# Weights packed on the host in the order of the ring, one run of 4 KB per partition and load

## The reference

```
def hybrid_mixer(x, w_in, mix_scale, w_out, gdn_conv_w, ..., fox_f_bias):
    proj = jnp.einsum('btd,de->bte', x, w_in)          # w_in 1024 x 3218
    ...                                                # delta rule, convolutions, attention
    mixed = jnp.concatenate([o_a, o_b, o_c], axis=-1) * mix_scale
    return jnp.einsum('bte,ed->btd', mixed, w_out)     # w_out 1024 x 1024

def swiglu(x, w1, w3, w2):                             # dense: 1024 x 2816, 2816 x 1024
    h = jax.nn.silu(jnp.einsum('btd,df->btf', x, w1)) * jnp.einsum('btd,df->btf', x, w3)
    return jnp.einsum('btf,fd->btd', h, w2)

def moe_swiglu(x, w_router, w1, w3, w2):               # 8 experts: 1024 x 3584, 3584 x 1024
    ...
    def expert_block(args):
        xb, e = args
        h = jax.nn.silu(xb @ w1[e]) * (xb @ w3[e])
        return h @ w2[e]
```

## Time and profile before

| | before |
|---|---|
| median of 3 runs | 2567.8 us (2567.65 to 2568.49) |
| profiled execution: span | 2567.1 us |
| PE busy | 2380.6 us (93%) |
| DVE busy, ACT busy | 1618.7 us, 1226.7 us |
| DMA | 536.82 MB in 421,484 packets, 209 GB/s over the span |
| queue of SP (q1) | 61.0% of the 16 engines' time |
| chain that ended last | PE 85%, DVE 7%, ACT 3%, issue 3%, DMA 1% |

### The profile page before, as it was taken

How to read it: one execution, slowest core, us unless ns; L and a number is a source line. 1 busy time by engine, 2 the same in 40 slices (tenths; PEclk the granted TensorE clock), 3 DMA queues, 4 the chain that set the end, 5 groups by cost and what they waited for, 6 DMA issues and landing times.

```text
span 2567.1 us, 31674 instructions
## 1 busy us (share of the span) xinstructions
PE 2380.6 (93%) x11343; PEld 1937.9 (75%) x11343; DVE 1618.7 (63%) x1855; ACT 1226.7 (48%) x1315; POOL 188.2 (7%) x224
## 2 busy tenths in 40 slices
PE   7988899898879999999999999999699999997997
PEld 6777688785867878787877777778488778756886
DVE  3564554265548888888888888888654407523443
ACT  1222244104117777777777786867543312222432
POOL 2020000012120000000000000000290001000000
PEclk9998899999879999999999999999899989878999
DMA  7400555440019989898999998999456444223552
GB/s 253 128 1 1 164 180 180 142 153 27 1 41 343 364 309 362 307 365 307 364 307 357 305 367 304 364 312 365 152 182 196 152 153 143 99 70 103 180 181 80
DMA packets 421484, 536.82 MB, mean 209 GB/s; under 512 B 20126, under 2 KB 379432, under 8 KB 421288
## 3 DMA queue, kind: packets, MB, share of 16 engines
q1 hardware_dynamic: 414928, 523.21, 61.0%
q0 software_dynamic: 3168, 9.86, 1.2%
q10 hardware_dynamic: 3320, 2.82, 0.3%
HBM read 532.67 MB, written 3.15 MB: 209 GB/s over the span
## 4 chain that ended last, share of the span: by engine, by line
PE 85%; DVE 7%; issue 3%; ACT 3%; ACTq 1%; DMA 1%; DVEq 0%; POOL 0%; SPq 0%
PE bank L991 18%; PE bank L992 18%; PE bank L993 18%; PE bank L808 5%; PE bank L1164 4%; PE bank L968 2%; PE bank L1012 1%; PE bank L804 1%; PE bank L1074 1%; PE bank L1312 1%; PE bank L907 1%; PE bank L918 1%; PE bank L921 1%; PE bank L767 1%; PE bank L1295 1%
## 5 line engine op out<-in xcount | busy, mean ns | idle before, releaser
L1749 DVE TENSOR_TENSOR weights_lo<-ring_data,weights_hi 128x2048 fp32r<-128x2048 f32 x435 | 995.7, 2303 | 176.5 <-ACT weights_hi L1363 175.9
L1363 ACT ACTIVATE weights_hi<-ring_data 128x2048 fp32r<-128x2048 f32 x435 | 825.8, 1915 | 91.9 <-DMA ring_data<-in_moe_w 90.7
L991 PE MATMUL bank<-weights_hi,xg_hi 128*128 128x512 f32 x896 | 365.5, 408 | 1.5 <-DVE xg_lo L2094 1.5
L993 PE MATMUL bank<-weights_hi,xg_lo 128*128 128x512 f32 x896 | 353.5, 395 | 0.0
L992 PE MATMUL bank<-weights_lo,xg_hi 128*128 128x512 f32 x896 | 353.0, 394 | 0.0
L991 PE MATMUL bank<-weights_hi,hT_hi 128*128 128x512 f32 x712 | 282.7, 397 | 16.4 <-DVE hT_lo L1761 16.4
L1338 ACT ACTIVATE arena<-bank 128x384 f32<-128x384 f32 (+4 forms) x186 | 93.8, 523 | 426.7 <-PE bank L808 111.8
L992 PE MATMUL bank<-weights_lo,hT_hi 128*128 128x512 f32 x712 | 283.5, 398 | 0.0
L993 PE MATMUL bank<-weights_hi,hT_lo 128*128 128x512 f32 x712 | 279.4, 392 | 0.0
L1374 ACT ACTIVATE hT_hi<-bank 128x256 fp32r<-128x256 f32 x178 | 65.0, 384 | 346.0 <-PE bank L1012 345.6
L991 PE MATMUL bank<-weights_hi,xT_hi 128*128 128x512 f32 x528 | 214.8, 407 | 16.3 <-issue 16.3
(11 more groups left out here) (423 smaller groups left out, 2856.4 us busy)
## 6 DMA issues: line engine op xcount, KB each, us to landing
ring_data<-in_moe_w SPq DMA_DIRECT2D x672, 512.0 KB, 4.7
ring_data<-in_ffn_w_in SPq DMA_DIRECT2D x88, 512.0 KB, 4.7
ring_data<-in_w_in SPq DMA_DIRECT2D x70, 512.0 KB, 4.6
ring_data<-in_ffn_w SPq DMA_DIRECT2D x66, 512.0 KB, 4.2
ring_data<-in_ffn_w_out SPq DMA_DIRECT2D x44, 512.0 KB, 4.2
ring_data<-in_w_out SPq DMA_DIRECT2D x24, 512.0 KB, 4.4
ring_data<-in_w_in SPq DMA_DIRECT2D x8, 396.0 KB, 4.5
ring_data<-in_w_in SPq DMA_DIRECT2D x8, 390.0 KB, 6.7
```

The lines of the kernel that those rows point to most:

```text
L991: mm(o, x_hi, w_hi, start=start, stop=False, **kw)
L993: return mm(o, x_lo, w_hi, start=False, stop=stop, **kw)
L1363: nc.scalar.activation(f.hi_slot(f.n0 + at), f.ring.slot(f.n0 + at), ACT.Copy).then_inc(f.ring.hi_done, 1)
L1749: v.tensor_tensor(f.lo_slot(f.n0 + at), w, f.hi_slot(f.n0 + at), ALU.subtract).then_inc(f.ring.lo_done, 1)
```

## The change

The host writes all streamed weights into two arrays, `stream1` (first block) and `stream2` (second block), in the order in which the ring takes them. Each slot is 128 rows of 8 KB, row p holding what partition p gets, in the layout that the slot had before (narrow blocks are padded with zeros that are not loaded). `Ring.load` takes the slot's rows and issues two halves, each one run per partition: 4096 bytes for a full slot, 3168 or 3120 for the blocks of 198 and 195 columns. An up slot's halves were `w1` and `w3` before; now they are the first and the second two row blocks, with both weights in each. The number of DMAs, their sizes, the ring, the waits and everything on the other engines stay.

```diff
-    def load(self, sp, n, dst, src, more=0):
+    def load(self, sp, n, src, w=8 * FC, more=0):
...
-        half = dst.shape[1] // 2
-        if isinstance(src, tuple):
-            parts = [(dst[:, :, FC * i:FC * i + FC], src[i]) for i in range(2)]
-        else:
-            parts = [(dst[:, half * i:half * i + half, :], src[:, half * i:half * i + half, :]) for i in range(2)]
-        for d, r in parts:
-            sp.dma_start(d, r).then_inc(self.loaded[n % RING], 16)
+        slot, half = self.slot(n), w // 2
+        for i in range(2):
+            r = slice(half * i, half * i + half)
+            sp.dma_start(slot[:, r], src[:, r]).then_inc(self.loaded[n % RING], 16)
...
+            def slot_of(ring, n):
+
+                return a[("stream1", "stream2")[ring is ring2]][bass.ds(n * P, P), :]
...
-                    ring.load(sp, n0 + m, ring.slot(n0 + m)[:, 0:8 * w].rearrange("p (k c) -> p k c", k=DT), cols(a["w_in"][l], c, w))
+                    ring.load(sp, n0 + m, slot_of(ring, n0 + m), 8 * w)
...
+def slot_rows(w, c, n):
+
+    return w[:, c:c + n].reshape(-1, P, n).transpose(1, 0, 2).reshape(P, -1)
...
+def stream(slots):
+
+    out = np.zeros((len(slots), P, 8 * FC), np.float32)
+    for n, v in enumerate(slots):
+        out[n, :, 0:v.shape[1]] = v
+    return out.reshape(-1, 8 * FC)
```

More of the change, by code:

```diff
@@ L528, in rest, with dense @@
                     chunk(c, 0, r)
[L529 to L536, removed]
+                down(f, 0, f.down_at(f.chunks - 1), r, e)
+            def dense(f):
+                first(f)
+                rest(f)
             mixer(0)
-            dense(ffn, a["ffn_w1"][0], a["ffn_w3"][0], a["ffn_w2"][0])
+            dense(ffn)
             mixer(1)
-            w1, w3, w2 = (a[k].rearrange("o e d f -> (o e d) f") for k in ("moe_w1", "moe_w3", "moe_w2"))
             def expert(part, e, it):
-                part(experts, lambda c, half: w1[bass.ds(e * D + 512 * half, 512), bass.ds(c * FC, FC)],
-                     lambda c, half: w3[bass.ds(e * D + 512 * half, 512), bass.ds(c * FC, FC)],
-                     lambda c: w2[bass.ds(e * FE + c * FC, FC), :], it * (MOE_LOADS // RING))
+                part(experts, it * (MOE_LOADS // RING), e * MOE_LOADS)
             expert(first, 0, 0)
@@ L557, in _ @@
             ring2.before = lambda n: sp.wait_ge(ring.used, npass * (E * MOE_LOADS) + (n_moe + n + 1 - RING))
[L559 to L577, removed]
+            dense(ffn1)
+            for n in range(N_MEM, N_FFN2):
+                m = n - N_PROJ2
+                w = 8 * PROJ2[m][1] if 0 <= m < len(PROJ2) else 8 * FC
+                ring2.load(sp, n, slot_of(ring2, n), w)
+            dense(ffn2)
             for j in range(TT):
@@ L2386, with dense_slots, up, streams @@
 w_o_m_2 w_out_2 ffn2_norm_2 ffn2_w_in_2 ffn2_w_out_2 final_norm_2""".split()
+def slot_rows(w, c, n):
+    return w[:, c:c + n].reshape(-1, P, n).transpose(1, 0, 2).reshape(P, -1)
+def dense_slots(w1, w3, w2):
+    def up(c):
+        for half in range(2):
+            r, f = slice(512 * half, 512 * half + 512), slice(FC * c, FC * c + FC)
+            yield np.stack([w[r, f].reshape(4, P, FC) for w in (w1, w3)], 2).transpose(1, 0, 2, 3).reshape(P, -1)
+    chunks = w2.shape[0] // FC
+    yield from up(0)
+    for c in range(1, chunks):
+        yield from up(c)
+        yield slot_rows(w2[FC * (c - 1):FC * c], 0, D)
+    yield slot_rows(w2[FC * (chunks - 1):], 0, D)
+def stream(slots):
[3 more added lines that the diff above has]
+    return out.reshape(-1, 8 * FC)
+def streams(i):
+    one, two = [], []
+    for l in range(DEPTH):
+        one += [slot_rows(i["w_in"][l], c, w) for c, w, _ in PROJ]
+        one += [slot_rows(i["w_out"][l], FC * m, FC) for m in range(OUT_LOADS)]
+        if l == 0:
+            one += dense_slots(i["ffn_w1"][0], i["ffn_w3"][0], i["ffn_w2"][0])
+    for e in range(E):
+        one += dense_slots(i["moe_w1"][0, e], i["moe_w3"][0, e], i["moe_w2"][0, e])
+    for k in ("ffn1", "ffn2"):
+        w = i[f"{k}_w_in_2"][0]
+        two += dense_slots(w[:, 0:FFN], w[:, FFN:], i[f"{k}_w_out_2"][0])
+        if k == "ffn1":
+            two += [slot_rows(i["w_mem_kv_2"][0], FC * m, FC) for m in range(2)]
+            two += [slot_rows(i["w_in_2"][0], c, w) for c, w, _ in PROJ2]
+            two += [slot_rows(i["w_o_a_2"][0], 512 * m, 512) for m in range(2)]
+            two += [slot_rows(i["w_o_m_2"][0], 0, D)]
+            two += [slot_rows(i["w_glu_2"][0], D * (1 - m), D) for m in range(2)]
+            two += [slot_rows(i["w_out_2"][0], FC * m, FC) for m in range(4)]
+    return {"stream1": stream(one), "stream2": stream(two)}
+STREAMED = """w_in w_out ffn_w1 ffn_w3 ffn_w2 moe_w1 moe_w3 moe_w2 ffn1_w_in_2 ffn1_w_out_2 w_in_2 w_o_a_2 w_glu_2
+w_mem_kv_2 w_o_m_2 w_out_2 ffn2_w_in_2 ffn2_w_out_2""".split()
 def kernel(**inputs):
@@ L2394 @@
     arrays, args = {}, {}
-    laid = {k: np.ascontiguousarray(inputs[k]) for k in NAMES}
+    laid = {k: np.ascontiguousarray(inputs[k]) for k in NAMES if k not in STREAMED}
+    laid.update(streams({k: np.asarray(inputs[k]) for k in STREAMED}))
     laid["consts"] = np.concatenate(list(shape_constants().values()), 1)
```

21 lines of the change are left out of this document (10 added, 11 removed).

## The result

The changed kernel takes 2622.5 us (median of 4 runs, 2619.6 to 2631.7) against 2567.7 us for the kernel before in the same rounds: a ratio of 1.0222, with a 95% interval of 1.0204 to 1.0240. That is 54.7 us more; forecast were 5.4. The profiled execution took 2622.2 us, with a span of 2620.4, so the traces can be compared as they stand: 53.3 us lie between the two spans.

The account below looks back on a forecast made before the run. PE was taken to bound the kernel, busy 93% of the span, with loads mostly hidden in the experts. Gate +4.5, clock +2.7, experts -1.8 gave +5.4 us on 2567.8: 2573.2 us, range 2564 to 2577.

Parts of the forecast that it names:

- the pricing of the loads in the experts: Experts: engines' work per load falls 14%, late loads catch up; 1.8 us gained, between 0 and 2.3.
- near 0.85: Experts: sign that the DMA share falls from 0.98 to near 0.85.
- The queue sum: Start, before PE's gate: ring 16.3, constants' delay 0.6, parameters 3.3, POOL 2.6, sum 22.8 us; with idle time 26.6.
- 37.7: Start: time in us when PE's gate, waiting for all parameter loads, would open, 4.5 us later than before.
- the upper end (+6.1): Start: the gate 6.1 us later if the ring's packets are stretched by a tenth where queues meet.
- the third rival: Start: small packets wait and stretch more, gate at 41 or later; +7 or more, 2575 to 2578 us; chance 0.1.
- the first rival: Start: queues take turns by bytes, gate opens 1.7 to 4 us earlier; 2562.0 to 2564.3 us; chance 0.2.
- The clock: Start: PE idles over 10 us, then runs 5.4 us behind the gate at 0.50; 2.7 us of work lost.
- the late loads that the prediction priced: Middle six experts: two disturbed ones stand 1.5 and 0.4 us over the level, others up to 0.2; 1.8 us gained.
- the level of 130.95: Experts: time in us of an undisturbed expert, taken to stay because it is PE's own matmuls.
- its signs of being wrong: Line 814 starting before 33.35, the clock staying at 1.00 there, or an expert under 130.9 us.
- The dense networks: Dense networks and mixers after the first: no DMA holds PE, so shorter loads are worth nothing.

Follow-up runs that it names:

- crossed halves: Changed kernel with the halves stored the other way round in every second row, so a load takes blocks 0 and 3, or 1 and 2: 2580.1 us, ratio 1.0047.
- the kernel before with the hold: Kernel before the change, with SP waiting before slot 3 until all parameter loads have landed: 2567.4 us, ratio 0.9994.

## Why the prediction was wrong

**The step that failed** is the pricing of the loads in the experts. The prediction took 159 ns for a run of 4096 bytes from a queue alone, let the engines' work on a load fall by 14%, and concluded that "a load that comes late has room to catch up": 1.8 us gained, between 0 and 2.3, with no loss in the range. The row is of POOL's layer norm parameters, one row of 4 KB that goes to all 128 partitions, and its price was carried over to packets that lie 8 KB apart. What the runs showed in its place: between 900 and 1690 us half a slot lands in 5.6 us instead of 4.7, and the experts lose 44.4 us. The same packets at a pitch of 4 KB give 130.7 us an expert; with crossed halves, 131.3. What in the chip's memory makes the difference was not shown. The runs only show that it goes with the parity of the 4 KB block.

The engines' mean work was not the whole of it. By the durations of the packets between 900 and 1690 us, four of 1024 bytes took 201 ns before, and one of 4096 takes 185 ns in the changed kernel and 176 at a pitch of 4 KB. The median of the 4096-byte packets is 159 ns in both, as priced; one in a hundred takes 662 ns or more in the changed kernel, and 508 at a pitch of 4 KB. So the work on a load did fall, by 8%, and the load landed later all the same. The forecast went from the mean work straight to the time of a load, and the two came apart.

The rows also held a warning that was read as comfort. ACT waited for a load 0.7 us each time, in all experts, and the prediction set this aside because PE stayed busy. A reading that fits the chain of the changed kernel, but was not tested by itself: the way from a freed slot back to PE had no slack in ACT's part, so that a load that lands 1 us later is 1 us later for DVE and, once DVE has used up its lead, for PE. ACT's waits, forecast to shrink to under 20 us, grew to 153.5. At a DMA share of 0.98 a loss had to be priced as well as a gain. The share of "near 0.85" was off too: it is 0.91, in the changed kernel and at a pitch of 4 KB alike.

The Trainium skill has a rule of this kind in DMA: Bandwidth & Descriptors (Latency and other measured facts): copies between tensors in HBM are slower at row pitches of large powers of two (207 GB/s at 512 KiB, 103 at 4 MiB), and padding by 4 KiB restores the rate (214). It should have been weighed. It gives no figure for a pitch under 512 KiB, so it would not have priced 8 KB; here 8 KB costs (136.7 us an expert against 130.7), and a padding of 1 KB is enough (130.9).

**What held.** The start went as forecast in its steps. The ring's packets took one turn each against those of the constants and the parameters (80 to 82 and 364 to 363). The queue sum was 16.3 us for the ring, 3.3 for the parameters and 2.6 for POOL; measured from 12.17 to 39.7 they are 60.0%, 11.7% and 9.4% of 27.5 us, that is 16.5, 3.2 and 2.6. The constants landed 1.0 us later instead of 0.6, and 5.2 us were idle instead of 3.8: together the 2 us by which the gate (39.7) missed 37.7. This is just beyond the upper end (+6.1), at +6.4, where the third rival begins, though it came more by idle time than by stretched packets: 6.46 MB in 16.5 us is 167 ns for 4096 bytes, 5% over the price. In the variants with 4 KB runs at other pitches the gate opens between 40.5 and 42.0. Loading the first blocks as before, or holding the ring back, takes the delay away (34.1 and 29.0), so its cause is shown. The rule of turns by bytes, the first rival, is out also for single runs of 4096 bytes from SP: 364 to 363.

The clock fell to 0.50 over PE's 14 us of idle time, as forecast, but came back after 3.67 us of work and not 5.4: line 788 begins at 47.05 instead of 38.89, 8.2 us late, of which the gate is 6.4 and the clock 1.8, where 2.7 had been put down. The experts begin 9.0 us late where 4.5 + 2.7 = 7.2 had been the sum; the last 0.8 us have no cause shown.

**The gain in the experts** was real, and hidden under the loss: where the pitch is harmless, six experts take 130.7 us instead of 131.3 each, 3.6 us in six where 1.8 had been put down. Of this, 2.2 us are the late loads that the prediction priced. The other 1.4 come from the level of 130.95 itself, which it had put at nothing because it is "PE's own matmuls": PE's busy time in an expert falls from 128.0 to 127.8 us. An expert of less than 130.9 us was one of its signs of being wrong.

Had the halves been stored apart, the forecast (2573.2) would have met the time (2572.0), but partly by luck. In that variant's trace the experts begin 9.8 us late (7.2 forecast), all eight take 3.7 us less (1.8 forecast), and the part behind them 3.9 us less (nothing forecast). This last part varies from one execution to the next whatever the layout: 750.0 us before and 749.9 after, but 743.6 in the kernel before with the hold.

**The dense networks** were rightly put at nothing. The first takes 187.2 us (292.79 to 480.02) where it took 188.5 (284.53 to 472.98), at 171 GB/s and with the 8 KB pitch in all its loads. So the pitch costs nothing there, where the ring has room to spare.

## What to carry to other kernels

A load's packet price holds for its addresses too: before a layout is changed, write down which 4 KB blocks one load touches, and let them be contiguous, or at least even and odd; halves of a row go into one load, or are stored apart. Where a stream uses 98% of the DMA engines and the next engine already waits a little for each load, price a slower load as carefully as a faster one, through every engine on the way. And longer packets on a bulk queue push back small loads on another; if the program waits for the small ones, hold the bulk back until they have landed, which here was worth some 11 us. Last, the mean work of the engines on a load does not tell when the load lands; take the landing from a run with the layout that is meant.

## What the runs showed of the hardware

- Loads of 128 runs of 4 KB: 369 GB/s with runs 4 KB apart, 320 to 363 in 20 us stretches with runs 8 KB apart, all in 4 KB blocks of one parity. At 16 KB apart it was little worse (an expert 1.4%), at 9 or 12 KB apart there was almost nothing left of it.
- The median packet of 4096 bytes took 159 ns at a pitch of 4, 8 or 16 KB. The mean was 176 ns at a pitch of 4 KB, 185 at 8 KB and 190 at 16 KB, and half a slot landed after 4.0, 5.6 and 5.8 us.
- Contiguous loads of 1 KB runs stood at 348 GB/s in the middle of an expert, at a DMA share of 1.10, and kept it at 134.4 us; 4 KB runs ran at up to 369, and 4 KB and 8 KB runs both reached 130.7.
- While they had packets waiting, two hardware queues and the software queue took one packet each in turn, whether it had 32, 1024 or 4096 bytes (875 to 899 in the earlier trace rows, 364 to 363 now; with POOL's, 126, 133 and 130 in the earlier trace rows).
